# Attention: a group's transposes ahead of its projection piece in TensorE's order

## What is computed

```python
qkv = hl @ w_qkv                       # latent tokens; kv_c = hc @ w_qkv[:, D:] for the context
s_win = einsum(q_r, k_win) * scale + bias     # window of 8 rows x 16 columns of the grid
s_ctx = einsum(q_r, k_ctx) * scale            # all 256 context tokens
p = softmax(concatenate([s_win, s_ctx]))
o = einsum(p_win, v_win) + einsum(p_ctx, v_ctx)
yl = o @ w_o
```

## Time and profile before

| what | value |
|---|---|
| median of 3 runs | 2870.51 us (2864.2 to 2871.42) |
| the profiled execution | 2871.17 us |
| its span, first to last instruction | 2869.4 us |
| mean granted clock of TensorE | 0.988 |
| PE busy | 2758.6 us (96%) |
| DVE, ACT, POOL busy | 67%, 33%, 38% |
| attention, pairs 0 to 7 | from about 1616 to 2046 us of the span |

### The profile page before, as it was taken

One profiled execution on the slowest core, in us unless ns is written; L12 is line 12 of the kernel. 1 busy time (PEld: TensorE's weight loads), 2 busy tenths in 40 slices (PEclk: granted clock), 3 DMA queues, 4 the chain that ended last, 5 costly groups with the idle time before them and its releaser, 6 DMA issues.

```text
span 2869.4 us, 42078 instructions
## 1 busy us (share of the span) xinstructions
PE 2758.6 (96%) x14290; PEld 2287.9 (80%) x14290; DVE 1933.0 (67%) x2826; ACT 952.4 (33%) x1678; POOL 1094.4 (38%) x792
## 2 busy tenths in 40 slices
PE   6999999899999999999999999999899999999998
PEld 3888888677788888889988788888777778888885
DVE  4777675777777777764765356556547877777777
ACT  4211111522222222234641366666413222222223
POOL 1212111124756556510001345455312575656552
PEclk9999999999999999999999999999999999999999
DMA  6322221031111111168567556556830111111111
GB/s 246 119 67 68 85 69 30 21 132 52 45 58 51 50 52 51 51 227 277 171 200 195 164 182 189 163 179 180 281 102 26 48 52 51 51 55 47 51 58 66
DMA packets 192341, 305.98 MB, mean 107 GB/s; under 512 B 61424, under 2 KB 125936, under 8 KB 192240
## 3 DMA queue, kind: packets, MB, share of 16 engines
q1 hardware_dynamic: 192240, 304.64, 32.8%
HBM read 255.28 MB, written 52.82 MB: 107 GB/s over the span
## 4 chain that ended last, share of the span: by engine, by line
PE 82%; DVE 4%; issue 3%; SPq 3%; ACT 3%; DMA 2%; POOL 2%; ACTq 0%; DVEq 0%; POOLq 0%
PE psum L1283 22%; PE psum L1135 19%; PE psum L1094 16%; PE psum L1468 6%; PE psum L1333 4%; PE psum L1421 3%; PE psum L1344 2%; PE psum L1527 2%; PE psum L1121 2%; PE psum L1498 2%; PE psum L1512 1%; ACT probs L2014 1%; SPq L662 1%; DVE residual L2239 1%; SPq L602 1%
## 5 line engine op out<-in xcount | busy, mean ns | idle before, releaser
L2239 DVE SCALAR_TENSOR_TENSOR residual<-psum,modulation,residual 128x512 f32<-128x512 f32 x896 | 639.5, 729 | 387.1 <-PE psum L1135 383.7
L2780 POOL TENSOR_TENSOR w_lo<-raw,w_hi 128x1024 fp32r<-128x1024 f32 x118 | 297.1, 2526 | 919.1 <-ACT w_hi L1655 914.4
L1135 PE MATMUL psum<-prod_hi,w_hi 128*128 128x512 f32 x896 | 350.2, 391 | 15.2 <-DVE residual L2239 10.5
L1135 PE MATMUL psum<-prod_lo,w_hi 128*128 128x512 f32 x896 | 343.5, 383 | 0.0
L1135 PE MATMUL psum<-prod_hi,w_lo 128*128 128x512 f32 x896 | 343.3, 383 | 0.0
L2813 POOL TENSOR_TENSOR w_lo<-raw,w_hi 128x512 fp32r<-128x512 f32 x175 | 259.4, 1482 | 209.6 <-ACT w_hi L1818 209.6
L1655 ACT ACTIVATE w_hi<-raw 128x1024 fp32r<-128x1024 f32 x186 | 194.0, 1057 | 429.4 <-PE psum L1094 173.2
L1283 PE MATMUL psum<-act_hi,w_hi 128*128 128x512 f32 x700 | 273.5, 391 | 6.1 <-POOL w_lo L2813 5.9
L1283 PE MATMUL psum<-act_hi,w_lo 128*128 128x512 f32 x700 | 272.6, 389 | 0.0
L1283 PE MATMUL psum<-act_lo,w_hi 128*128 128x512 f32 x700 | 272.5, 389 | 0.0
L1135 PEld LDWEIGHTS psum<-prod_hi,w_hi 128*128 128x128 f32 x896 | 168.3, 188 | 74.6 <-DVE residual L2239 33.9
(11 more groups left out here) (262 smaller groups left out, 6167.5 us busy)
## 6 DMA issues: line engine op xcount, KB each, us to landing
raw<-ffn_panels SPq DMA_DIRECT2D x198, 512.0 KB, 3.3
raw<-conv_panels SPq DMA_DIRECT2D x32, 512.0 KB, 6.0
rest_in<-mod_rest SPq DMA_DIRECT2D x40, 384.0 KB, 4.3
more_row<-mod_panels SPq DMA_DIRECT2D x48, 256.0 KB, 2.7
v_st<-v_dram SPq DMA_DIRECT2D x32, 320.0 KB, 4.8
mod_in<-mod_rest SPq DMA_DIRECT2D x24, 384.0 KB, 5.8
mod_early<-mod_panels SPq DMA_DIRECT2D x16, 512.0 KB, 15.2
raw<-qk_panels SPq DMA_DIRECT2D x16, 512.0 KB, 5.7
```

What stands on the lines that cost most here:

```text
L1135: mm = pe.matmul(psum[:, 6 + r % 2 if bank is None else bank, 0:tn], w[:, s, ob, :], h[:, t0:t0 + tn], start=(n == 0), stop=(n == 2))
L2239: dve.scalar_tensor_tensor(out=residual[:, ob, t0:t0 + tn], in0=psum[:, 6 + r % 2 if bank is None else bank, 0:tn], scalar=modulation[:, g ...
L2780: pool.tensor_tensor(panel(w_lo, s), raw[:, s], panel(w_hi, s), ALU.subtract).then_inc(lo_done[s], 1)
```

## The change

In a group's step on PE, the call of `fill` moves from in front of the three branches of `turn` to behind them. Nothing else differs; every engine has the same instructions.

```diff
@@ -1550,13 +1550,13 @@
                                 scores(i, u + 2, g)
                             elif not last:
                                 scores(i + 1, u + 2 - UNITS, g)
-                        fill(i, group0[u] + g, reach)
                         if g + 2 < n:
                             turn(i, u, g + 2)
                         elif u < UNITS - 1:
                             turn(i, u + 1, g + 2 - n)
                         elif not last:
                             turn(i + 1, 0, g + 2 - n)
+                        fill(i, group0[u] + g, reach)
                         values(i, u, g)
```

## The result

The changed kernel takes 2904.41 us (median of 4 runs, 2903.06 to 2904.8) against 2870.32 before (4 runs): ratio 1.0124, 95% interval 1.0109 to 1.0138. That is 34.1 us more; 31.2 were forecast, as 2901.7. The spans of the two profiled executions differ by 2903.0 - 2869.4 = 33.6.

What follows compares the result with a forecast made beforehand. PE was taken to bound the kernel, with 82% of the chain of waits. Four places in seven pairs (26.3) and one in six (5.0) gave 31.2 us on the median 2870.51: 2901.7 us, own range 2893 to 2912.

Steps and rivals of the forecast that it cites:

- What bounds the stage: Attention stage: PE holds 82% of the chain of waits; the change adds no matmul and moves only PE's standing still.
- What sets pt_lo: Five groups per pair: pt_lo hangs on the finished projection tile's copy, so issuing transposes earlier brings it forward by nothing.
- The five places: Groups 5, 9, 14, 18 and next pair's 0 cost 1.14, 1.00, 1.25, 0.36 and 0.83 us; together 31.2 us.
- wait of T(7): Group 5: the transposes of group 7 wait 1.14 us for pt_lo, previously hidden by the projection piece.
- V(9) behind the tile's end: Group 9: its values matmuls start 5.16 us after the tile's end, against 4.52 before; cost 1.00 us.
- PE's way from the tile's end: PE's time from tile's end to next piece, less 0.36 for transposes: 1.86 us left at group 5, 1.67 at 9.
- What was costed at nothing: Fourteen more transposes per pair move ahead of a piece, taken as 0; one losing its cover would cost 8.0 us.
- The clock: PE in the pairs: idle some 7.4 us in 60, yet clock loss costed at nothing; rival of 2922, chance 0.05.
- Waits removed: Rival at the five places: earlier transposes bring pt_hi and o_sum forward, gaining 19 us, giving 2852; chance 0.08.
- Given back: Rival: lateness from groups 5 and 14 comes off at 9 and 18; cost 14.5 us, giving 2885; chance 0.09.
- one for one: Rival: the transposes' wait replaces that of the values matmuls, nothing left over: 0, giving 2870.5; chance 0.04.
- What would show it: Changed profile: pair 60.2 us, same busy time, four or five pt_lo waits per pair, 1.1 to 1.7 us each.

Runs made afterwards that it cites:

- the run with the groups that end a tile: Kernel before, with transposes ahead of the projection piece only at groups 3, 7, 12, 16 and 22: 2878.64 us, ratio 1.0034.
- the run on two tiles: Changed kernel, with only the tiles ending at groups 3 and 12 copied later on ACT and DVE, at groups 5 and 14: 2885.3 us, ratio 1.0054 to before.

## Why the prediction was right

*What bounds the stage.* Right: PE's work and the clock stayed, the time went into PE's standing still in seven pairs.

*What sets pt_lo.* Right, and shown: with the copy moved behind pt_hi, and nothing else, the waits on pt_lo vanish from the list; with the copy where it was, pt_lo of group 5 ends 2.95 us behind the tile in both orders.

*The five places.* Forecast and measured in pair 2; the last column takes the time from the tile's end to the next tile's end, with the change less before. (The ends are taken as in the prediction, from the start of what follows: 1751.24, 1762.95, 1775.73, 1787.46 and 1799.31 with the change. The stretch of group 0 runs into the next pair.)

| group | what was forecast | forecast | measured | cost forecast | cost measured |
|---|---|---|---|---|---|
| 5 | wait of T(7) | 1.14 | 1754.24 - (1752.56 + 0.48) = 1.20 | 1.14 | 11.71 - 10.50 = 1.21 |
| 9 | V(9) behind the tile's end | 5.16 | 1768.23 - 1762.95 = 5.28 | 1.00 | 12.78 - 11.69 = 1.09 |
| 14 | wait of T(16) | 1.25 | 1778.73 - (1777.15 + 0.25) = 1.33 | 1.25 | 11.73 - 10.36 = 1.37 |
| 18 | V(18) behind the tile's end | 4.48 | 1791.94 - 1787.46 = 4.48 | 0.36 | 11.85 - 11.49 = 0.36 |
| 0 | V(0) behind the tile's end | 4.78 | 1804.23 - 1799.31 = 4.92 | 0.83 | 12.49 - 11.59 = 0.90 |

(0.48 and 0.25 are the lengths of the V in front, from start to start before.) Per pair 4.58 were forecast and 4.93 came: 0.28 x 7 + 0.07 x 6 = 2.4 of the missing 2.9 us. The rest is smaller than the spread of the runs.

The term that was mis-sized is PE's way from the tile's end. The first matmul behind transposes is followed later than others: V's second came 0.20 behind the first at 1739.60, where the transposes stood in front of V, and 0.12 at 1751.24, where the piece does. The piece pays it instead: 0.32 from 1766.77 to 1767.09, against 0.23 before (1751.77 to 1752.00). The rows of before:

```profile
1739.80 0.28 PE L1527 MATMUL psum<-pt_lo,v_st 128*128 128x256 f32 x1
...
1752.00 0.40 PE L1468 MATMUL psum<-act_lo,w_hi 128*128 128x512 f32 x1
```

PE's sum is unchanged. But about 0.08 us moved from behind the tile's end, where it lay over the wait, to a place where it covers nothing, at four of five places. (The prediction took 0.36 out of PE's way for the transposes and left the rest as it was.) At group 18 V hangs on o_sum, and the forecast holds to 0.01. The same 0.08 is what the run with the groups that end a tile had beyond its 0.36, at each of its three places.

*What was costed at nothing.* Right for the changed kernel, by luck in one place: at group 10 the cover falls short by 0.6 us, and only the wait at group 9 hides that, by some 0.02 us. The prediction asked what covers pt_hi and pt_lo and left out that the first transposes of a unit wait for POOL, too. The waits list of before could not show it, as that wait did not exist. The distance from the releaser's end to the start would have: before, POOL's probabilities ended at 1756.01 and T(12) started at 1756.81, so 0.80 us were to spare, and the piece that went from in front of T(12) had taken 1.38.

```profile
1754.54 1.47 POOL L2924 TENSOR_SCALAR probs<-probs,stats 128x512 f32<-128x512 f32 x2 [0.28 <-POOL table L2916]
...
1756.81 0.60 PE L1512 MATMUL psum<-ident,probs 128*128 128x128 f32 x4
```

*The clock.* PE's idle rose to 11% of a pair (53.68 busy of 60.56) and the granted clock stayed 1.00. So the rule of the Trainium skill on micro-idles (TensorE: Matmul & The Clock Gate, "A second HAM failure mode: psum-queue depth-cycling") did not bite here.

*The rivals.* "Waits removed" fell with the order alone, but its mechanism is real once its condition is met: with the copy out of pt_hi's way the same order gives 2853.41, where the rival had 2852. A pair is 2.78 us shorter than before, and the waits that stood there came to 2.8. "Given back" fell with the run on two tiles, "one for one" with the waits at groups 5 and 14.

*What would show it.* The pair (60.2 forecast, 60.56 measured) and the waits on pt_lo came as written, with 0.96 to 1.7 us by the records where 1.1 to 1.7 were forecast. The wait on o_sum at group 18 has no idle in the records any more, though V(18) still starts 0.06 behind the end of o_sum (1791.46 + 0.42): the modelled ends of F(18) cover it.

## What to carry to other kernels

Independent work in front of an instruction that waits is cover; moving the waiting instruction ahead pays only if what it waits for gets earlier by it. Ask of each wait which event it hangs on: here an in-order copy on ACT and DVE tied a transposition's buffer to the end of an unrelated matmul group, and both the loss (12 parts in 1000) and the later gain (6 in 1000) came from that copy's place in the queue. Two reorderings that each lose or do nothing can win together, so try the pair before dropping either.

## What was not expected of the hardware

The first matmul behind a run of 128 x 128 transposes takes some 0.08 us longer to the next start (0.20 against 0.12 for a 256-column matmul, 0.32 against 0.23 for a 512-column one); it goes along with the transposes wherever they are put, and does not change PE's sum. It is not a matter of transposes alone: a piece behind V's matmuls of 128 columns has 0.28 in the same place (1757.42 to 1757.70 before), 0.05 more than one behind scores (0.23). What causes it stays open. The trace shows this much beside it: behind transposes the weights of V's second matmul begin to load 0.08 us after the first matmul's start (1739.60 to 1739.68), and behind a piece they begin with it (1751.24).
